# Expert rows added back as two fp32r parts behind the selections, and GpSimd's piece copy cut into four instructions of 512 columns

## The chip, the cores and the metric

The kernel runs on one core of a Trainium2 chip. The metric is the time of one launch in device microseconds: the median of three runs before is 1791.22 us (1789.27 to 1792.38). Lower is better.

## The reference

Two transformer blocks run one behind the other, all in float32, for one sequence of 256 tokens (16 meta tokens in front in the first block) of width 1024. The first block is a SwiGLU feed-forward, a mixer (stick-breaking attention and latent attention, each projected, gated and mixed by `w_out`) and a second SwiGLU. The second block is modulated by a condition vector and has a mixer (causal convolution and forgetting attention) and a mixture of 32 experts, four for each token. What matters here of the first mixer and of the experts:

```python
    g = jax.nn.sigmoid(gate_pre + b_gate)
    g_sb, g_mla = g[..., :D_MODEL], g[..., D_MODEL:]
    out = (g_sb * y_sb + g_mla * y_mla) @ w_out
    ...
    def expert_block(args):
        xi, e = args
        hc = xi @ w1[e] + b1[e]
        g, u = hc[:, :D_EXPERT], hc[:, D_EXPERT:]
        g = jnp.minimum(g, SWIGLU_LIMIT)
        u = jnp.clip(u, -SWIGLU_LIMIT, SWIGLU_LIMIT)
        hm = (u + 1.0) * (g * jax.nn.sigmoid(SWIGLU_ALPHA * g))
        return hm @ w2[e] + b2[e]
    ...
    y = jax.ops.segment_sum(yb.astype(jnp.float32) * gate_buf[:, None], tok_buf, num_segments=T)
```

After the experts comes the residual `x + g2 * y` and a last RMS norm with the gain `final_g`.

## The kernel before, in words

Each engine has its own program in one block, written out by hand, and they meet at semaphores. There is no scheduler: an engine does its instructions in the order of the text.

**Dense layers.** Activations lie with features on the 128 partitions and tokens in the columns. Weights come as a stream of pieces of 2048 columns (`PIECE`, 1 MB), into a ring of six slots on the SP queue. For precision a product is made as three fp32r products (lines 750 to 752): high and low parts of weights and inputs. ScalarE makes the high part of a piece (`split_piece`, L1537, into `w_hi`), VectorE the rest (`rest`, L2019, into `w_lo`; in the second mixer GpSimd, L1946). The table `BUF` says which of the buffers of `w_hi` and `w_lo` a piece takes. `split_piece` waits on `freed` for the last piece in the same buffer.

In the first mixer the attention ends with `MIX1_OUT`: eight pieces, four for the projections `o1` (two tiles of output columns a piece, 24 products a tile) and four for `w_out` (`w1`). VectorE's `gated` (L2324, L2325, L2327) multiplies the two projections of a tile by their gates and adds them, ScalarE copies the high part (`x_hi`, L1746), and VectorE makes the lower part (`x_lo`, L2071). ScalarE opens the gates by two sigmoids a tile (L1678, L1679). TensorE may begin tile m of `o1` when tile m - 2 is gated. `y_hi`, `y_lo`, `t_a` and `mtmp` lie in ring slots that double as the third weight buffer.

**Experts.** After routing, tokens are gathered in blocks of 64 slots. There is a block an expert, or more for one with more than 64 tokens. An expert's weights are 12 pieces, eight for `w_exp_in` and four for `w_exp_out`. SP loads them in pairs of 2 MB into four staging places (`stage_own`, `stage_conv`, `stage_gates`, `stage_norms`, L645), when GpSimd has emptied the place. GpSimd copies each piece into its slot of the ring of twelve (L1970), when it has landed and TensorE has freed the slot. The loops of TensorE (L1437), ScalarE (L1899) and VectorE (L2607) run over blocks.

A block on TensorE: bias (L1443), first layer for k = 0 to 3 (L1388), rows of the block before added back for half of the outputs (`back_to_tokens`, L1400), k = 4 to 7, the other half, the gather of the next block's tokens (L1366), transposes (L1457, L1378, L1464), and the second layer (L1477). Adding back is a product of the expert's output `ye` (64 slots on each half of the partitions) with the selection `ST` (slots by tokens, holding the gate's weight at the token of a slot), both fp32. ScalarE copies `ST` (L1910) and `ye` (L1912) out of PSUM. VectorE makes the selections `S` (L2572) and `SG` (L2614), one-hot rows for the bias (L2576), adds the sums to `acc` (`add_up`, L2583), and clips and multiplies the hidden layer. Behind the loop lie the last two adds, residual, squares, the norm's sum and root, and eight products by gain and root (L2642).

## Time and profile before

| | us |
|---|---|
| median of three runs | 1791.22 |
| profiled execution | 1787.52 |
| its span, first to last instruction | 1785.7 |
| PE busy | 1725.7 (97%) |
| DVE busy | 971.7 (54%) |
| POOL (GpSimd) busy | 840.2 (47%) |
| ACT busy | 528.4 (30%) |
| median from issue to landing of a staged pair | 15.4 |

PE is TensorE's matmuls, PEld its weight loads, SPq the transfers' queue. The span is time on the device between the first and the last instruction, and the profiled time has 1.8 us around it. A busy time sums the durations of an engine's instructions; for matmuls the ends are modelled, so they overlap. The HBM traffic is 560 MB, of which the experts' weights are 403 MB.

### The profile page before, as it was taken

How to read it: one execution, taken by the hardware profiler on the slowest of the kernel's cores; microseconds unless marked ns; L12 is line 12 of the kernel's file. 1: busy time of each engine (PE TensorE's matmuls, PEld its weight loads, DVE VectorE, ACT ScalarE, POOL GpSimd, SP SyncE). 2: the span in 40 equal slices, each digit the busy share in tenths (PEclk: the TensorE clock that was granted, in tenths of full speed). 3: DMA queues.
4: the chain of work that ended last, by engine and by line, in shares of the span. 5: the costliest groups of instructions: out<-in, count | busy, mean ns of one | idle time of the engine just before them, and what ended most of it. 6: DMA issues, size and time to landing. Idle time of an engine off the chain costs nothing.

```text
span 1785.7 us, 29478 instructions
## 1 busy us (share of the span) xinstructions
PE 1725.7 (97%) x10968; PEld 1097.3 (61%) x10969; DVE 971.7 (54%) x1438; ACT 528.4 (30%) x830; POOL 840.2 (47%) x492
## 2 busy tenths in 40 slices
PE   8999998998999999999999999999999999999997
PEld 8999996888899988898433333333333333333333
DVE  6777664576777666966654344334444435444334
ACT  6444444645644455573110110110101011010111
POOL 0000011000000038675677777777777768777773
PEclk9999999999999999999999999999999999999999
DMA  9767633225276625349799999999999999999994
GB/s 370 278 253 294 230 119 129 108 104 215 108 282 258 239 100 218 132 142 363 294 429 429 428 428 428 428 428 429 428 428 428 428 424 430 428 429 429 428 429 180
DMA packets 55262, 560.44 MB, mean 314 GB/s; under 512 B 6208, under 2 KB 7360, under 8 KB 14400
## 3 DMA queue, kind: packets, MB, share of 16 engines
q1 hardware_dynamic: 54912, 559.50, 77.1%
q8 instruction: 43, 0.70, 0.2%
q14 instruction: 19, 0.16, 0.0%
q10 hardware_dynamic: 288, 0.07, 0.0%
HBM read 558.50 MB, written 1.05 MB: 313 GB/s over the span
## 4 chain that ended last, share of the span: by engine, by line
PE 61%; DMA 22%; ACT 5%; DVE 5%; issue 4%; POOL 3%; POOLq 0%; SPq 0%; DVEq 0%; ACTq 0%
DMA stage_conv<-w_exp_in 14%; PE bank L1388 13%; PE bank L750 11%; PE bank L752 10%; PE bank L751 10%; DMA stage_conv<-w_exp_out 7%; PE bank L1477 6%; POOL ring L1970 3%; PE bank L1400 2%; PE bank L1366 2%; ACT w_hi L1537 1%; DVE bank L2000 1%; DMA ring<-stream 1%; PE bank L877 1%; PE bank L1378 1%
## 5 line engine op out<-in xcount | busy, mean ns | idle before, releaser
L1388 PE MATMUL bank<-ring,arena 128*64 128x512 f32 x2112 | 472.7, 596 | 11.5 <-POOL ring L1970 11.0
L750 PE MATMUL bank<-x_hi,w_hi 128*128 128x256 f32 (+1 forms) x1336 | 383.8, 287 | 18.5 <-DVE x_lo L2000 6.0
L752 PE MATMUL bank<-x_hi,w_lo 128*128 128x256 f32 (+1 forms) x1336 | 378.9, 284 | 0.0
L751 PE MATMUL bank<-x_lo,w_hi 128*128 128x256 f32 (+1 forms) x1336 | 378.5, 283 | 0.0
L1388 PEld LDWEIGHTS bank<-ring,arena 128*64 128x64 f32 x2112 | 143.4, 136 | 304.6 <-issue 243.0
L1946 POOL TENSOR_TENSOR w_lo<-ring,w_hi 128x512 fp32r<-128x512 f32 x104 | 135.1, 1334 | 386.4 <-ACT w_hi L1537 386.4
L750 PEld LDWEIGHTS bank<-x_hi,w_hi 128*128 128x128 f32 x1336 | 251.9, 189 | 26.6 <-issue 13.0
L752 PEld LDWEIGHTS bank<-x_hi,w_lo 128*128 128x128 f32 x1336 | 252.2, 189 | 0.0
L751 PEld LDWEIGHTS bank<-x_lo,w_hi 128*128 128x128 f32 x1336 | 251.4, 188 | 0.2
L1537 ACT ACTIVATE w_hi<-ring 128x2048 fp32r<-128x2048 f32 (+1 forms) x123 | 224.4, 1825 | 87.6 <-PE bank L750 83.1
L2019 DVE TENSOR_TENSOR w_lo<-ring,w_hi 128x2048 fp32r<-128x2048 f32 x91 | 208.1, 2286 | 75.1 <-ACT w_hi L1537 75.0
L1477 PE MATMUL bank<-ring,arena 128*64 128x512 f32 x1056 | 232.2, 592 | 0.0
L1970 POOL COPY ring<-stage_own 128x2048 f32<-128x2048 f32 x94 | 175.4, 1895 | 82.5 <-PE bank L1388 50.9
L1970 POOL COPY ring<-stage_conv 128x2048 f32<-128x2048 f32 x94 | 175.8, 1893 | 55.1 <-DMA stage_conv<-w_exp_in 23.2
L1970 POOL COPY ring<-stage_norms 128x2048 f32<-128x2048 f32 x92 | 171.9, 1893 | 62.1 <-DMA stage_norms<-w_exp_in 23.2
L1970 POOL COPY ring<-stage_gates 128x2048 f32<-128x2048 f32 x92 | 171.6, 1894 | 43.1 <-DMA stage_gates<-w_exp_in 21.6
L2576 DVE TENSOR_SCALAR onehot<-cst 96x64 bf16<-96x64 f32 x66 | 66.0, 1000 | 204.6 <-PE bank L1400 204.6
L1901 ACT ACTIVATE cst<-cst 128x512 f32<-128x512 f32 x33 | 20.8, 629 | 504.0 <-DVE cst L2004 504.0
L1477 PEld LDWEIGHTS bank<-ring,arena 128*64 128x64 f32 x1056 | 74.0, 137 | 136.1 <-issue 128.6
L2572 DVE TENSOR_SCALAR arena<-cst,small 128x64 f32 x66 | 68.2, 1076 | 139.1 <-issue 139.1
L1925 POOL TENSOR_TENSOR arena<-x_hi,x_lo 128x128 f32<-128x128 f32 x1 | 2.4, 2447 | 226.6 <-DVE x_lo L2000 226.6
L752 PE MATMUL bank<-hid_hi,w_lo 128*128 128x272 f32 (+1 forms) x352 | 100.0, 284 | 0.0
(384 smaller groups left out, 2225.8 us busy)
## 6 DMA issues: line engine op xcount, KB each, us to landing
ring<-stream SPq DMA_DIRECT2D x119, 1024.0 KB, 5.6
stage_own<-w_exp_in SPq DMA_DIRECT2D x31, 2048.0 KB, 15.4
stage_conv<-w_exp_in SPq DMA_DIRECT2D x31, 2048.0 KB, 15.4
stage_gates<-w_exp_in SPq DMA_DIRECT2D x31, 2048.0 KB, 15.4
stage_norms<-w_exp_in SPq DMA_DIRECT2D x31, 2048.0 KB, 15.4
stage_own<-w_exp_out SPq DMA_DIRECT2D x16, 2048.0 KB, 15.4
stage_conv<-w_exp_out SPq DMA_DIRECT2D x16, 2048.0 KB, 15.4
stage_gates<-w_exp_out SPq DMA_DIRECT2D x15, 2048.0 KB, 15.4
```

Of the source, the lines that this page charges most:

```text
L750: begin = mm(out_, wh, xh, start=start, stop=False)
L751: mm(out_, wh, xl, start=False, stop=False)
L752: return begin, mm(out_, wl, xh, start=False, stop=stop)
L1366: last = mm(to[pr, :], S[:, t, :], h2n[:, t, 512 * j:512 * j + 512], start=(t == 0), stop=(t == 1), tile_position=pos)
L1388: last = mm(bank[2 + gu][pr, :], xT[:, k % 4, k // 4, :], ring[:, k, c0:c0 + 512], start=False, stop=(k == KD - 1), tile_position=pos)
L1477: last = mm(bank[5][pr, :], hmT[:, k % 4, k // 4, :], ring[:, s, c0:c0 + 512], start=False, stop=(k == KD - 1), tile_position=pos)
L1537: last = A(w_hi[:, BUF[p], part * n:part * n + n], ring[:, p % RING, part * n:part * n + n], ACT.Copy)
L1946: nc.gpsimd.tensor_tensor(w_lo[:, BUF[p], c:c + REST_COLS], ring[:, p % RING, c:c + REST_COLS], w_hi[:, BUF[p], c:c + REST_COLS].bitcast(f32),
L1970: nc.gpsimd.tensor_copy(ring[:, j, :], stage[pair % PLACES][:, j % 2, :]).then_inc(in_place, 1)
L2019: tt(w_lo[:, BUF[p], :], ring[:, p % RING, :], w_hi[:, BUF[p], :].bitcast(f32), ALU.subtract)\
L2572: last = V.tensor_scalar(S[:, t, :], slots(b_), slot[:, t, bass.ds(e_, 1)], None, ALU.is_equal)
L2576: return V.tensor_scalar(to[0:3 * E, :], const("ones", 0, SLOT_TOK, 3 * E), cst[0:3 * E, bass.ds(e_ + CONST["eye3"][0], 1)], None, ALU.mult)
```

## The change

1. `BUF` for the first mixer's gates and outputs takes three buffers in turn. What lay in the third (`t_a`, `t_a_meta`, `mtmp`) and in the twelfth ring slot (`y_hi`, `y_lo`) now lies in `stage_own`.
2. ScalarE splits `MIX1_OUT[1]` ahead of the last `pair_evac`, and `MIX1_OUT[2]` behind three of the eight pairs of sigmoids. VectorE's `rest` of the following piece stands beside a gated tile, ahead of the lower parts. The first two tiles of `w1` are made together, k by k.
3. Adding rows back is two fp32r products: `ye_hi` and `ye_lo` against `ST`, which now holds ones. The gate's weight is taken up by `ye` as a factor a slot (`row_gate`, the row sum of the selection). VectorE makes `row_gate` and `ST` at the block's end, and `ye_lo` (`lower_rows`) behind the selections `S` and `SG`. TensorE waits for `m_yl` ahead of the add.
4. Behind the loop, `acc` takes up residual and gate first, the sums are added from PSUM, the gain is multiplied in ahead of the root, and two products of 1024 columns with the root follow.
5. GpSimd copies a piece in four instructions of 512 columns; the last one signals.

```diff
-for _p in MIX1_GATES:
-    BUF[_p] = (_p - MIX1_GATES[0] + 1) % 2
-BUF.update(zip(MIX1_OUT, (1, 0, 1, 0, 1, 0, 1, 2)))
+BUF.update(zip(MIX1_GATES, (1, 0, 1, 2, 0, 1, 2, 0)))
+BUF.update(zip(MIX1_OUT, (1, 2, 0, 1, 2, 0, 1, 2)))
...
@@ TensorE
-            for m in range(KD):
-                if m >= 2:
-                    pe.wait_ge(evac["w1"], m - 1)
-                tile(cur, bank[4 + m % 2][:, 0:SEQ], (lambda k: split_x(k, 0, SEQ)) if m else
-                     lambda k: split_x_first("w1", k, 0, SEQ), KD, proj)
+            two_tiles(cur, [bank[4 + i][:, 0:SEQ] for i in range(2)], "w1", w_lower, ORDER[cur.b // BLK] + 1)
+            for m in range(2, KD):
+                pe.wait_ge(evac["w1"], m - 1)
+                tile(cur, bank[4 + m % 2][:, 0:SEQ], lambda k: split_x(k, 0, SEQ), KD, proj)
...
                     for j, _, pr in halves:
-                        mt = 2 * r + mp
-                        last = mm(bank[banks[j]][:, mp * 256:mp * 256 + 256], ye[pr, mt * P:mt * P + P],
-                                  ST[pr, :, :].rearrange("p a b -> p (a b)"),
-                                  start=True, stop=True, tile_position=(64 * j, 0))
+                        to = bank[banks[j]][:, mp * 256:mp * 256 + 256]
+                        mm(to, ye_hi[pr, mt * P:mt * P + P], ST[pr, :], start=True, stop=False,
+                           tile_position=(64 * j, 0))
+                    for j, _, pr in halves:
+                        to = bank[banks[j]][:, mp * 256:mp * 256 + 256]
+                        last = mm(to, ye_lo[pr, mt * P:mt * P + P], ST[pr, :], start=False, stop=True,
+                                  tile_position=(64 * j, 0))
...
-                pe.wait_ge(m_ys, g + 1)
+                pe.wait_ge(m_yl, g + 1)
...
@@ ScalarE
+            split_piece(MIX1_OUT[1])
+            use(ACT.Sigmoid)
             pair_evac(3, yy_hi, soft["mla"]["pv"], soft["mla"]["y"])
-            split_piece(MIX1_OUT[1])
-            open_gates("gates", graw)
+            open_gates("gates", graw, range(0, 3))
+            split_piece(MIX1_OUT[2])
+            open_gates("gates", graw, range(3, KD))
             for m in range(KD):
                 if m % 2 == 0 and m:
-                    split_piece(MIX1_OUT[m // 2 + 1])
+                    split_piece(MIX1_OUT[m // 2 + 2])
...
-                act.wait_ge(m_xt, g + 2)
-                act.wait_ge(m_comb, g * 2 + 2)
-                A(ST[:, :, :].rearrange("p a b -> p (a b)"), bank[0][:, 0:256], ACT.Copy).then_inc(m_sts, 1)
+                act.wait_ge(m_sts, g + 2)
                 act.wait_ge(m_y, g + 1)
-                A(ye, bank[5][:, :], ACT.Copy).then_inc(m_ys, 1)
+                A(ye_hi[:, :], bank[5][:, :], ACT.Copy, scale=row_gate).then_inc(m_ys, 1)
...
@@ GpSimd
-                    nc.gpsimd.tensor_copy(ring[:, j, :], stage[pair % PLACES][:, j % 2, :]).then_inc(in_place, 1)
+                    for c in range(0, PIECE, MOVE_COLS):
+                        last = nc.gpsimd.tensor_copy(ring[:, j, c:c + MOVE_COLS],
+                                                     stage[pair % PLACES][:, j % 2, c:c + MOVE_COLS])
+                    last.then_inc(in_place, 1)
...
@@ VectorE
                     if m:
                         then(m - 1)
+                    beside(m)
                 then(KD - 1)
...
+            def lower_rows(g):
+
+                dve.wait_ge(m_ys, g + 1)
+                stt(ye_lo[:, :], bank[5][:, :], row_gate, ye_hi[:, :].bitcast(f32), ALU.mult, ALU.subtract)\
+                    .then_inc(m_yl, 1)
...
+                lower_rows(g)
                 dve.wait_ge(m_comb, g * 2 + 1)
...
+                V.reduce_sum(row_gate, bank[0][:, 0:256], AX.X)
+                ts(ST[:, :], bank[0][:, 0:256], 0.0, None, ALU.is_gt).then_inc(m_sts, 1)
+            dve.wait_ge(m_acc, n_blocks * 2 + 1)
+            for m in range(KD):
+                mark(stt(acc[:, m, :], acc[:, m, :], mod[:, 40 + m:41 + m], real(res[:, m, :]), ALU.mult, ALU.add))
+            lower_rows(n_blocks)
...
+            for half in range(2):
+                four = slice(half * KD // 2, (half + 1) * KD // 2)
+                tt(fin[:, four, :], acc[:, four, :], rstd[:, 0:SEQ].unsqueeze(1).to_broadcast([P, KD // 2, SEQ]),
+                   ALU.mult).then_inc(fin_ready, KD // 2)
```

The order on ScalarE at the start of the output projections, before:

```order
L1707 ACTIVATE y_mla_hi<-bank 128x256
L1537 ACTIVATE w_hi<-ring 128x2048
L1512 ACT_TABLE_LOAD
L1678 ACTIVATE arena<-arena,col 128x256
L1679 ACTIVATE arena<-arena,col 128x256
...
L1746 ACTIVATE x_hi<-arena 128x256 x2
L1537 ACTIVATE w_hi<-ring 128x2048
```

And of the change (lines from here on are ten higher on this engine: L1547 is the split, L1688 and L1689 the sigmoids):

```order
L1547 ACTIVATE w_hi<-ring 128x2048
L1522 ACT_TABLE_LOAD
L1717 ACTIVATE y_mla_hi<-bank 128x256
L1688 ACTIVATE arena<-arena,col 128x256
L1689 ACTIVATE arena<-arena,col 128x256
...
L1547 ACTIVATE w_hi<-ring 128x2048
L1688 ACTIVATE arena<-arena,col 128x256
L1689 ACTIVATE arena<-arena,col 128x256
...
L1759 ACTIVATE x_hi<-arena 128x256 x2
L1547 ACTIVATE w_hi<-ring 128x2048
```

The first split went ahead of the last y, the second from behind sixteen sigmoids and two x_hi to behind six sigmoids.

VectorE at the same place, before:

```order
L2019 TENSOR_TENSOR w_lo<-ring,w_hi 128x2048
L2324 TENSOR_TENSOR ring<-bank,arena 128x256
L2325 TENSOR_TENSOR ring<-bank,arena 128x256
L2327 TENSOR_TENSOR arena<-ring 128x256
...
L2071 TENSOR_TENSOR x_lo<-arena,x_hi 128x256
L2019 TENSOR_TENSOR w_lo<-ring,w_hi 128x2048
L2324 TENSOR_TENSOR ring<-bank,arena 128x256
```

And of the change:

```order
L2031 TENSOR_TENSOR w_lo<-ring,w_hi 128x2048
L2336 TENSOR_TENSOR stage_own<-bank,arena 128x256
L2337 TENSOR_TENSOR stage_own<-bank,arena 128x256
L2339 TENSOR_TENSOR arena<-stage_own 128x256
L2031 TENSOR_TENSOR w_lo<-ring,w_hi 128x2048
...
L2083 TENSOR_TENSOR x_lo<-arena,x_hi 128x256
L2336 TENSOR_TENSOR stage_own<-bank,arena 128x256
```

The rest (L2019, now L2031) of the piece for columns 4 and 5 moved from behind the second gated tile and the first x_lo to directly behind the first gated tile.

VectorE in the loop over expert blocks, of the change: the selections, the lower rows, the one-hot row, the add to `acc`, and at the block's end the row sum and `ST`:

```order
L2583 TENSOR_SCALAR arena<-cst,small 128x64
L2633 ISA x2
L2633 TENSOR_SCALAR arena<-cst,small 128x64 x2
...
L2012 SCALAR_TENSOR_TENSOR ye_lo<-bank,small,ye_hi 128x512
L2635 ISA
L2587 ISA
L2587 TENSOR_SCALAR onehot_77<-cst 96x64
L2594 TENSOR_TENSOR arena<-arena,bank 128x512 x2
...
L2650 COPY arena<-bank 128x512
L2651 TENSOR_REDUCE small<-bank 128x1
L2016 TENSOR_SCALAR ST<-bank 128x256
```

Before, the three rows L2012, L2651 and L2016 were not there, and ScalarE copied `ST`.

## Rows read from the trace of the kernel before

**Rows 1.** The page: GB/s in the 40 slices; the expert matmuls of the first layer.
```profile
GB/s 370 278 253 294 230 119 129 108 104 215 108 282 258 239 100 218 132 142 363 294 429 429 428 428 428 428 428 429 428 428 428 428 424 430 428 429 429 428 429 180
L1388 PE MATMUL bank<-ring,arena 128*64 128x512 f32 x2112 | 472.7, 596 | 11.5 <-POOL ring L1970 11.0
```

**Rows 2.** Windows: length, busy us (records) of each engine, clock, DMA share, GB/s.
```profile
500.00:600.00 100.00, 100.00 (x848) 100.00 (x847) 70.80 (x89) 45.63 (x53) 0.00 (x0) 1.00 0.73 267
852.00:855.00 3.00, 2.49 (x32) 2.34 (x32) 1.89 (x9) 1.11 (x2) 0.00 (x0) 1.00 0.05 22
1600.00:1700.00 100.00, 99.66 (x502) 36.11 (x500) 38.50 (x57) 8.96 (x16) 76.00 (x41) 1.00 1.01 428
```

**Rows 3.** GpSimd's timeline, expert stage: start, us, what.
```profile
1656.41 3.73 POOL L1970 COPY ring<-stage_own 128x2048 f32<-128x2048 f32 x2 [1.16 <-PE bank L1477]
1661.30 3.73 POOL L1970 COPY ring<-stage_conv 128x2048 f32<-128x2048 f32 x2 [1.16 <-DMA stage_conv<-w_exp_in]
```

**Rows 4.** The chain that ended last: start, us, what.
```profile
1471.30 6.87 PE bank L1388 x32
1478.17 1.06 PE bank L1400 x8
...
1498.40 6.86 PE bank L1388 x31
...
1762.07 6.90 PE bank L1477 x32
```

**Rows 5.** Timeline of the end, GpSimd, ScalarE and VectorE.
```profile
1759.18 3.73 POOL L1970 COPY ring<-stage_conv 128x2048 f32<-128x2048 f32 x2 [1.14 <-DMA stage_conv<-w_exp_out]
...
1768.99 0.60 ACT L1912 ACTIVATE arena<-bank 128x512 f32<-128x512 f32 x1 [6.75 <-PE bank L1477]
...
1775.11 1.67 DVE L2000 SCALAR_TENSOR_TENSOR arena<-arena,small,res 128x256 f32<-128x256 f32 x4
...
1779.09 3.26 DVE L2000 SCALAR_TENSOR_TENSOR arena<-arena,col,rstd 128x256 f32<-128x256 f32 x8 [2.30 <-ACT rstd L1527]
```

**Rows 6.** Timeline of the first mixer's output projections.
```profile
404.12 0.49 ACT L1679 ACTIVATE arena<-arena,col 128x256 f32<-128x256 f32 x1
404.52 0.71 ACT L1746 ACTIVATE x_hi<-arena 128x256 fp32r<-128x256 f32 x2
405.13 1.90 ACT L1537 ACTIVATE w_hi<-ring 128x2048 fp32r<-128x2048 f32 x1
...
407.06 2.29 DVE L2019 TENSOR_TENSOR w_lo<-ring,w_hi 128x2048 fp32r<-128x2048 f32 x1 [1.68 <-ACT w_hi L1537]
...
410.54 0.39 PE L750 MATMUL bank<-y_sb_hi,w_hi 128*128 128x256 f32 x1 [4.27 <-DVE arena L2327]
...
431.13 0.36 PE L750 MATMUL bank<-x_hi,w_hi 128*128 128x256 f32 x1 [0.30 <-DVE w_lo L2019]
```

**Rows 7.** Groups by form, GpSimd: count, busy us, mean ns, idle before.
```profile
L1970 POOL COPY ring<-stage_conv 128x2048 f32<-128x2048 f32 x94 | 175.8, 1893 | 55.1 <-DMA stage_conv<-w_exp_in 23.2 <-DMA stage_conv<-w_exp_out 12.7 <-PE bank L1388 9.8
L1946 POOL TENSOR_TENSOR w_lo<-ring,w_hi 128x512 fp32r<-128x512 f32 x104 | 135.1, 1334 | 386.4 <-ACT w_hi L1537 386.4
L1933 POOL COPY arena<-arena 64x64 f32<-64x64 f32 x1 | 0.2, 235 | 0.1
```

**Rows 8.** Timeline of the first expert block, TensorE, VectorE and the transfers' queue.
```profile
862.91 0.33 SPq L645 DMA_DIRECT2D stage_own<-w_exp_out  x1
...
863.21 0.73 PEld L1400 LDWEIGHTS bank<-arena 64*128 64x128 f32 x8 [0.81 <-issue]
863.52 1.40 DVE L2572 TENSOR_SCALAR arena<-cst,small 128x64 f32 x2 [4.70 <-issue]
...
864.84 2.62 DVE L2614 TENSOR_SCALAR arena<-cst,small 128x64 f32 x4
...
871.28 0.36 SPq L645 DMA_DIRECT2D stage_gates<-w_exp_in  x1
...
879.30 0.34 SPq L645 DMA_DIRECT2D stage_norms<-w_exp_in  x1
```

More of the change, by code:

```diff
@@ L224, in build @@
         slot_bytes = PIECE * 4
-        stage = [at_place("stage_own", [P, 2, PIECE])[0],
+        stage_own, own_at = at_place("stage_own", [P, 2, PIECE])
+        own = stage_own[:, :, :].rearrange("p a b -> p (a b)")
+        stage = [stage_own,
                  at_place("stage_conv", [P, 2, PIECE], over=arena_at)[0],
@@ L290, in build @@
         gate = sm_area.take(2, E)
+        row_gate = sm_area.take(1)
         slot = sm_area.take(2, E)
@@ L574, in build @@
         m_y = sem("m_y")
-        m_ys = sem("m_ys")
+        m_ys = sem("m_y_high")
+        m_yl = sem("m_y_lower")
         m_comb = sem("m_comb")
@@ L1481, in _ @@
                 last.then_inc(m_y, 1)
-            pe.wait_ge(m_ys, n_blocks + 1)
+            pe.wait_ge(m_yl, n_blocks + 1)
             pe.wait_ge(m_sts, n_blocks + 1)
@@ L2314, in _, with gated @@
             rest(MIX1_OUT[1])
-            def gated(n, gr, tmp, to, then=lambda m: None):
+            def gated(n, gr, tmp, to, then, beside=lambda m: None):
                 for m in range(KD):
```

83 lines of the change are left out of this document (42 added, 41 removed).

## The prediction

> **What bounds the kernel now.** I read the page first [rows 1]: from the 21st of 40 slices on its line of GB/s stands flat at 424 to 430. So there are two regimes: up to about 852 us the dense layers, bound by TensorE, and then the 32 experts. In the windows [rows 2] the dense feed-forward issues 848 matmuls in 100 us, 0.118 us apart and at full clock, the DMA engines rest between 852 and 855 us (share 0.05, all places full), and in the expert stage they are busy throughout (share 1.01 from 1600 to 1700 us), where VectorE works 38.5 of 100 us; TensorE's 99.66 there say little, since the ends of matmuls are modelled. The GpSimd timeline [rows 3] then gives the beat of the expert stage: two pieces (one pair, 2 MB) are copied every 4.89 us, 3.73 us of it busy and 1.16 us idle until the next pair lands. Twelve pieces make an expert, so an expert takes 29.4 us, set by the transfers. TensorE alone needs 27.1 us for a block (1471.30 to 1498.40 in the chain, [rows 4]). It falls a block behind at the one expert that has two blocks (33 blocks in all: the 2112 records of L1388 in rows 1 are 64 a block) and makes up 2.3 us a block from there. At the end it still lags: the last pair's copy starts at 1759.18 and ends at 1762.91 [rows 5], while the last layer's matmuls, begun at 1762.07, run until 1768.97 [rows 4]. Behind the last piece only a quarter of that layer has to follow, 1.72 us, so the lag is 1768.97 - (1762.91 + 1.72) = 4.3 us. From 1768.97 to the end of the span, 16.7 us are a tail in which nothing else runs.
>
> **The change, part by part.**
>
> **1. First mixer, output projections.** Before [rows 6], ScalarE runs all sixteen sigmoids, then x_hi at 404.52, and only then splits the piece for columns 4 and 5 (405.13, 1.90 us); VectorE stands behind that split (rest at 407.06, 2.29 us), its third gated tile comes behind that, and TensorE, which needs it, starts column 4 at 410.54 after 4.27 us idle. Further on it starts the third w1 tile at 431.13. Now the order is another, and w_hi/w_lo have three buffers instead of two in turn, so a split waits for no reader. I played the queues forward with durations of rows 6 (ACT split 1.90, sigmoids 0.40 apart, DVE rest 2.29, and, of three operations of 256 columns, a gated tile 1.3 with its waits) and 24 x 0.118 = 2.84 us of TensorE a tile. The split for columns 2 and 3 moves ahead of the last y evacuation; three sigmoid pairs end at 397.3, the split for columns 4 and 5 at 399.2, its rest at 401.5, the third gated tile at 405.3, before TensorE ends column 3 (405.8). Then 0.6 us of waiting at column 5 remains and 0.1 at column 7; o1 ends at 418.0. The first two w1 tiles now go together, k by k, so they start while x_split 6 and 7 (421.4, 422.2) are still to come, and end at 423.7; the third waits for ScalarE's evacuation (0.7 us) and starts at 424.4. That is **6.7 us** earlier than 431.13. Bounds: 4.3 (the one stall only) and 8. What TensorE does up to the next norm is unchanged, and a shift here moves everything behind it.
>
> **2. Rows added back, in the loop.** Eight records of 256-column fp32 took 1.06 us on the chain [rows 4], twice a block. Eight fp32r matmuls of 256 columns, in pairs on the two halves of the rows, would be 4 x 0.107 = 0.43 us if paired as before; unpaired 8 x 0.118 = 0.94. I take 0.6: a block falls from 27.1 to about 26.2 us. This buys nothing where transfers set the beat; it only has to remove the 4.3 us of lag, and twelve blocks behind the double one are enough for it with 0.4 us each. VectorE gains the row sum, the selection and the lower half (256, 256 and 512 columns; some 1.4 us a block, estimated from the 2.29 for 2048 in rows 6), ScalarE loses a copy; VectorE is idle for more than half of the stage [rows 2], so these hide. If that cover went, the next tokens' selection would be late next, and behind it TensorE's gather.
>
> **3. GpSimd's four copies.** One piece of 2048 columns took 1.893 us and the smallest warm copy (64 columns, 64 partitions) 0.235 [rows 7]: 0.836 ns a column and 0.18 us fixed. So 512 columns should last 0.61 us, 0.56 apart, because like instructions overlap by 0.05 us here (two large copies take 3.73, not 3.79, [rows 3]). A pair then costs 8 x 0.56 = **4.5 us against the beat of 4.89**. Lower bound 3.73 (overheads hidden), upper bound 8 x 1.33 = 10.7 from the two-input subtraction of 512 columns; I go by the copies, being the same operation. By the Trainium skill, GPSIMD Engine Reference, "Instruction dispatch", every instruction is broadcast and dispatched in software by each of the eight cores, which speaks against cutting one into four. With the fixed part paid in full and no overlap the pair would cost 4.9, just at the beat (by that rule). In the sum, the last pair comes into place 0.75 us later (4.5 for 3.73), and all others are hidden by the 0.4 us of slack.
>
> VectorE's small selections are why the copies are cut: its 64-column operations last 0.24 us alone, but 1.40 us for two and 2.62 for four while copies run [rows 8]. It mostly ends in time, so a shorter wait alone is worth nothing.
>
> **4. The first block, a new wait.** TensorE's row add now waits for the lower rows (m_yl), which VectorE makes behind its selections. In block 0 VectorE only reaches these at 863.52 and 864.84 [rows 8], after its registers are loaded, and TensorE starts the row add at 863.21. With the shorter copies the six selections end at 866.5 (six waits of at most 0.56), the subtraction at 867.2: a stall of 3.9 us, 3.5 net of the faster add. Queued behind it are the expert matmuls of k = 4 to 7, which free the slots GpSimd fills, and on the SP queue the transfers that wait for those copies, just when the DMA engines restart from idle. The issues at 862.91, 871.28 and 879.30 become about 863.7, 875.9 and 882.7. From the last on the stream is unbroken, so it ends 882.7 - 879.3 = **3.4 us** later. That is a real loss, as the stream has no slack anywhere behind.
>
> **5. End of the loop.** Last pair at 1759.18 + 3.4 = 1762.6, in place at 1767.1, last matmul at 1768.9; by the other path, from piece 7 through add, gather and the 6.9 us layer, 1769.1. Against 1768.97: **0.1 us later**, the lag of 4.3 being what pays for parts 3 and 4.
>
> **6. Tail.** From the last matmul: ScalarE's high half 0.63, VectorE's lower half 0.74, row add 0.75, eight 256-column operations 3.3 (the 3.26 of rows 5), squares, sum and root behind them 2.3 (1776.78 to 1779.09), then two products of 1024 columns at 1.14 (half of 2.29 in rows 6) and 3.3 for the last store (from 1782.35). Sum 13.3 against 16.7: **3.4 us saved**. The eight multiplications by the gain fit beside squares, sums and root (2 us against 2.3).
>
> **Sum**: -6.7 + 0.1 - 3.4 = **-10.0 us**. The profiled execution took 1787.52 us (span 1785.7 and 1.8 around), so 1777.5 for a like one; the median of the runs shown is 1791.22, 3.7 above it. I forecast the median: 1791.2 - 10.0 = **1781.2**.
>
> **The rivals.**
> - *The first block costs nothing.* The lower rows come in time, or the stream restarts as before. For it: the DMA engines have just drained, and part of the first issues is bound by the copies anyway. Against it: 863.21 is before 863.52. Then 3.5 more: 1777.7.
> - *The mixer gives only its large stall*, ScalarE's queue being late elsewhere. Some 5 us less: 1786.
> - *The stream cannot close up.* With 0.4 us slack a pair, any copy held up by VectorE opens a further gap in the restart; 6 to 7 us lost: 1788, about the same as before.
> - *GpSimd becomes the bound (the slower side).* Point of decision: 4.894 / 8 = 0.612 us from copy to copy. With a gap of 0.04 behind each in place of an overlap it is 0.65, a pair 5.2, and 186 pairs x 0.31 = 57 us less the 10 gained: 1838. For it: the margin is 8%, and VectorE's eight small operations an expert (0.24 each) may now hold up copies. By the Trainium skill, SBUF — State Buffer, "Who interferes with whom", the port pair of the two engines is locked for a whole instruction, whichever comes first; the 1.40 and 2.62 us agree on VectorE's side. Against it: pairs of copies take 3.73 whatever VectorE does, and even 8 x 0.24 = 1.9 us on top of 26.9 an expert stays under 29.4.
> - *The change does nothing on the path*: excluded only in the expert stage, whose beat I expect untouched.
>
> **How the numbers follow.** Forecast 0.50 (own range 1777 to 1785), no cost of the first block 0.15, smaller mixer gain 0.12, stream not closed 0.10, GpSimd the bound 0.13. A measurement of this kernel can tell about 0.2%, 3.6 us. The first three are faster, the fourth is split, the fifth slower: faster 0.78, same 0.08, slower 0.14. The range 1774 to 1789 takes in the first four with the bounds of part 1 (4.3 to 8) and leaves out GpSimd's case.
>
> **What would show it.** In the changed profile: no wait of some 4 us in o1 and the third w1 tile near 424; a TensorE wait of 3 to 4 us for ye_lo in the first block, and a second full stop of the DMA engines there; copies of 0.61 us, pairs of 4.5 every 4.89; row adds of some 0.6 us; a last layer that waits for GpSimd; 13 us from the last expert matmul to the end. Pairs that follow each other more than 4.9 us apart with GpSimd never idle would prove me wrong, as would a first block without that wait.

## The result and the profile after

The changed kernel takes 2017.9 us (median of 4 runs) beside 1790.2 us of the kernel before on the same chip: ratio 1.127, 95% interval 1.126 to 1.129. It is **227.7 us slower**; the forecast was 10 us faster, with a range up to 1789.

The page of the profiled execution (span 2016.6 us; GB/s in 40 slices of 50.4 us; first costliest group of section 5: line, engine, operation, shapes, count, busy us, mean ns, idle before):

```profile
PE 1764.1 (87%) x10968; PEld 1121.8 (56%) x10969; DVE 1284.1 (64%) x1545; ACT 518.2 (26%) x797; POOL 976.5 (48%) x1608
GB/s 370 266 252 287 172 104 126 105 199 171 290 240 147 188 126 147 334 336 325 368 345 347 373 322 371 334 355 378 321 368 331 220 371 374 324 367 336 354 353 21
L2587 DVE TENSOR_SCALAR onehot<-cst 96x64 bf16<-96x64 f32 x66 | 383.6, 5812 | 211.3 <-PE bank L1411 211.3
```

The flat 428 GB/s of [rows 1] have become 220 to 378, so the transfers no longer set the beat. TensorE has lost its load too: 85.4 of 100 us from 1600 to 1700 where it had 99.7 [rows 2]. What stands at the top is an operation that the prediction never priced by itself: VectorE's one-hot, 64 columns, now 5.8 us on average. The page of the kernel before has it at 1.0 us:

```profile
L2576 DVE TENSOR_SCALAR onehot<-cst 96x64 bf16<-96x64 f32 x66 | 66.0, 1000 | 204.6 <-PE bank L1400 204.6
```

GpSimd's groups by form, which the forecast did price:

```profile
L1980 POOL COPY ring<-stage_conv 128x512 f32<-128x512 f32 x376 | 212.6, 613 | 145.2 <-PE bank L1487 140.6 <-PE bank L1394 4.6
```

A copy lasts 0.613 us, as forecast (0.61), and eight of them 4.50 us, as forecast. GpSimd is not the bound: it stands idle for 8.8 or 9.4 us at a time in 29 blocks. What TensorE waits for (us in total, times, longest):

```profile
PE bank L1407 <- DVE arena L2594: 209.0, 29, 7.2
PE bank L1407 <- DVE ye_lo L2012: 5.6, 2, 3.9
```

One block in the changed kernel, VectorE first, then GpSimd, then TensorE (start us, us, what, idle before and its releaser):

```profile
1625.52 12.82 DVE L2587 TENSOR_SCALAR onehot<-cst 96x64 bf16<-96x64 f32 x1 [6.55 <-PE bank L1411]
1638.25 1.27 DVE L2594 TENSOR_TENSOR arena<-arena,bank 128x512 f32<-128x512 f32 x2
...
1613.76 4.50 POOL L1980 COPY ring<-stage_own 128x512 f32<-128x512 f32 x8
1618.21 4.51 POOL L1980 COPY ring<-stage_conv 128x512 f32<-128x512 f32 x8
1622.65 4.51 POOL L1980 COPY ring<-stage_gates 128x512 f32<-128x512 f32 x8
1627.11 4.50 POOL L1980 COPY ring<-stage_norms 128x512 f32<-128x512 f32 x8
1631.56 4.51 POOL L1980 COPY ring<-stage_own 128x512 f32<-128x512 f32 x8
1636.01 2.28 POOL L1980 COPY ring<-stage_conv 128x512 f32<-128x512 f32 x4
1647.67 0.61 POOL L1980 COPY ring<-stage_conv 128x512 f32<-128x512 f32 x1 [9.38 <-PE bank L1487]
...
1639.58 0.58 PE L1407 MATMUL bank<-ST,ye_hi 64*128 64x256 f32 x2 [7.22 <-DVE arena L2594]
```

This is the main part of the loss in one picture, a circle of three engines. The one-hot is issued at 1625.52, while GpSimd copies without a break, and ends at 1638.33, 0.05 us after the last copy (1636.01 + 2.28). It has stood across 22 boundaries between two copies, where [rows 8] had let every operation in at the first. Behind it on VectorE waits the sum (L2594), and for that TensorE's second row add, 7.2 us. TensorE frees no slots meanwhile, so GpSimd fills the ring and stops; only that lets VectorE in. While TensorE catches up, the staging places fill as well. So GpSimd finds four pairs ready when it resumes and again copies without a break, into the next one-hot: the state keeps itself going. 29 blocks have a one-hot of 12.8 us. From one expert to the next GpSimd now needs 35.5 and 36.1 us in turn where it needed 29.4, and from its first pair to its last 1122.3 us (854.28 to 1976.60) where it needed 900.0 (859.16 to 1759.18, the latter in [rows 5]): **+222.3 us, nearly all of the loss**. Once the circle broke: at the expert with two blocks GpSimd waited 24 us for a slot, and the next four one-hots took 0.25, 0.24, 0.70 and 2.48 us. Then came the one at 1625.52.

The wait of 7.2 us is not all that a block loses. Within each of these stops TensorE's granted clock falls to half (0.50, the level of 1.2 GHz) and stays there for a while behind it, for example from 1635.6 to 1645.6 and from 1673.1 to 1679.8 us, of which TensorE works for 6.0 and 4.1 us; between the two it is 1.00. By an estimate from these rows this costs 3.0 and 2.0 us a block. An undisturbed block of 26.3 us, the wait of 7.2 and these 2.5 on average make 36.0, beside the 35.5 and 36.1 measured. So more than a third of the 6.4 us by which a block exceeds the beat comes with the slow stretch. No run here takes the clock's part away by itself.

### The profile page after: what moved, and what is told of

It is laid out like the page before. It is cut to its first block, busy times and chain, and to the rows that moved or that the text cites. A ratio compares the mean times of both kernels' runs of the same rounds, so it can differ in the third digit from the quotient of the medians.

```text
span 2016.6 us, 30667 instructions
## 1 busy us (share of the span) xinstructions
PE 1764.1 (87%) x10968; PEld 1121.8 (56%) x10969; DVE 1284.1 (64%) x1545; ACT 518.2 (26%) x797; POOL 976.5 (48%) x1608
## 4 chain that ended last, share of the span: by engine, by line
PE 69%; DVE 14%; issue 11%; ACT 4%; DMA 1%; POOL 1%; DVEq 0%; SPq 0%; ACTq 0%
PE bank L1394 12%; PE bank L1487 11%; PE bank L757 10%; PE bank L759 10%; PE bank L758 10%; DVE onehot L2587 9%; PE bank L1372 5%; PE bank L1407 2%; DVE arena L2594 2%; PE bank L1411 1%; PE bank L1384 1%; DVE bank L2012 1%; DMA ring<-stream 1%; PE bank L1467 1%; ACT w_hi L1547 1%
## 5 line engine op out<-in xcount | busy, mean ns | idle before, releaser
L2587 DVE TENSOR_SCALAR onehot<-cst 96x64 bf16<-96x64 f32 x66 | 383.6, 5812 | 211.3 <-PE bank L1411 211.3
L1980 POOL COPY ring<-stage_conv 128x512 f32<-128x512 f32 x376 | 212.6, 613 | 145.2 <-PE bank L1487 140.6
L1980 POOL COPY ring<-stage_norms 128x512 f32<-128x512 f32 x368 | 208.1, 613 | 127.5 <-PE bank L1487 127.5
L757 PEld LDWEIGHTS bank<-x_hi,w_hi 128*128 128x128 f32 x1336 | 252.7, 189 | 24.4 <-issue 12.5
L2031 DVE TENSOR_TENSOR w_lo<-ring,w_hi 128x2048 fp32r<-128x2048 f32 x91 | 208.0, 2286 | 64.2 <-ACT w_hi L1547 63.9
L1547 ACT ACTIVATE w_hi<-ring 128x2048 fp32r<-128x2048 f32 (+1 forms) x123 | 224.4, 1825 | 83.1 <-PE bank L757 78.6
L1407 PE MATMUL bank<-ST,ye_hi 64*128 64x256 f32 x272 | 53.5, 402 | 214.6 <-DVE arena L2594 209.0
L1980 POOL COPY ring<-stage_own 128x512 f32<-128x512 f32 x376 | 211.8, 613 | 56.3 <-PE bank L1394 56.3
L1980 POOL COPY ring<-stage_gates 128x512 f32<-128x512 f32 x368 | 207.3, 613 | 0.5 <-PE bank L1394 0.5
L1407 PEld LDWEIGHTS bank<-ST,ye_hi 64*128 64x128 f32 x272 | 32.9, 238 | 271.1 <-DVE arena L2594 234.5
L1372 PE MATMUL bank<-arena 128*64 128x512 f32 x272 | 112.7, 977 | 0.0
## 6 DMA issues: line engine op xcount, KB each, us to landing
stage_own<-w_exp_out SPq DMA_DIRECT2D x16, 2048.0 KB, 10.2
```

The source lines that it names most:

```text
L757: begin = mm(out_, wh, xh, start=start, stop=False)
L1372: last = mm(to[pr, :], S[:, t, :], h2n[:, t, 512 * j:512 * j + 512], start=(t == 0), stop=(t == 1), tile_position=pos)
L1407: mm(to, ye_hi[pr, mt * P:mt * P + P], ST[pr, :], start=True, stop=False, tile_position=(64 * j, 0))
L1547: last = A(w_hi[:, BUF[p], part * n:part * n + n], ring[:, p % RING, part * n:part * n + n], ACT.Copy)
L1980: last = nc.gpsimd.tensor_copy(ring[:, j, c:c + MOVE_COLS], stage[pair % PLACES][:, j % 2, c:c + MOVE_COLS])
L2031: tt(w_lo[:, BUF[p], :], ring[:, p % RING, :], w_hi[:, BUF[p], :].bitcast(f32), ALU.subtract)\
```

## Experiments

All times are medians beside the kernel before on the same chip (1789.5 to 1790.4 us). Three questions: which part of the change costs, what shuts VectorE out, and how little removes it.

**1. whole_pieces: the change without the cut.**

```diff
-MOVE_COLS = 512
+MOVE_COLS = 2048
```

> The change with GpSimd's copies left whole (2048 columns), everything else of it kept. Theory L (lock-out): the loss comes from the cut alone. Copies of 512 columns follow each other so closely that VectorE's one-hot operation (96 x 64, to bf16) stands 12.8 us in 28 of 33 blocks, until the ring is full and GpSimd stops; TensorE waits 7.2 us for it (209 us in all). Whole copies let it in after 1.9 us at most, so the time is 1790.2 - 4.9 (dense layers, as measured) - 2.2 (tail, 14.5 for 16.7 us) + 0 to 3, so 1782 to 1786, and no wait of TensorE for the sum of VectorE's L2594 over 1 us. Theory R (row add): the new place of the lower rows moves the one-hot into a phase of the copies in which it loses; then whole copies also leave long one-hots (several times 1.9 us) and the time stays over 1820.

Measured: 1783.6 us, ratio 0.9966 (0.9952 to 0.9979). The one-hot in its profile:

```profile
L2587 DVE TENSOR_SCALAR onehot<-cst 96x64 bf16<-96x64 f32 x65 | 53.9, 829 | 171.2 <-PE bank L1411 171.2
```

Theory L holds. Everything else of the change together gains 6 us; the cut costs some 234.

**2. split_alone: the kernel before with only the copy cut into four.** The loop over four copies of 512 columns in place of the single copy, nothing else.

> The kernel before with nothing but the copy of a piece cut into four of 512 columns. Theory L: the one-hot operation stands until the ring is full here too, over 10 us in most blocks, and the time is 1950 to 2060. Theory R: without the new row add the one-hot waits for one copy of 0.61 us at most, the pairs take 4.5 us against a beat of 4.89, and the time is 1788 to 1793.

Measured: 2039.2 us, ratio 1.139 (1.137 to 1.141); 29 one-hots of 12.5 us, and TensorE waits 199.8 us for the sum. The new row add is not needed for the loss. Theory R is out.

**3. add_first: the addition ahead of the one-hot.**

```diff
                 dve.wait_ge(m_comb, g * 2 + 1)
-                one_hot(onehot2, e).then_inc(m_SG, 1)
                 dve.wait_ge(m_acc, g * 2 + 1)
                 add_up(0)
+                one_hot(onehot2, e).then_inc(m_SG, 1)
```

> The change with two steps of VectorE exchanged: the addition of the rows (from PSUM, two of 512 columns) goes ahead of the one-hot for the output bias. This moves the one-hot by about 1.2 us, so to another phase of the copies (0.556 us apart). Theory K (kind): an operation of this kind never gets in between two short copies, in whatever phase. Then it still stands for over 10 us in most blocks, TensorE now waits for hm instead of the sum, and the time stays at 1950 to 2060. Theory P (phase): the one-hot was locked out because it always came 0.08 us behind the start of a copy; in four blocks it came at 0.51 or 0.52 us and got in after 0.70. Then the long ones vanish in a part of the blocks or in all, and the time falls below 1900.

Measured: 1966.8 us. The one-hot still stood for 11.2 to 11.7 us in 29 blocks, and this at many phases of the copies (from 0.04 over 0.21 and 0.41 to 0.55 us behind a start). Phase does not decide. The stall fell less heavily because TensorE could go on to its second row add first: it now waits 148.5 us in all, ahead of the transposes, where it had waited 209.0 for the sum.

**4. onehot_float: the one-hot in fp32, turned to bf16 by ScalarE.** VectorE writes 96 x 64 fp32 into dead columns (the router's logits and mask), ScalarE copies them to `onehot1` and `onehot2`.

> The change with both one-hots written by VectorE as fp32 (as its selections are, which get in at every boundary of two short copies) and turned to bf16 by ScalarE. Theory K (the form of the operation, bf16 out, decides): no one-hot over 0.7 us, no wait of TensorE for the sum, time 1782 to 1788. Theory P (phase or place): VectorE's fp32 one-hot stands as long as the bf16 one did (12.8 us), time about 2018.

Measured: 2018.2 us, the same as the change to 0.3 us.

```profile
L2592 DVE TENSOR_SCALAR arena<-cst 96x64 f32<-96x64 f32 x65 | 385.9, 5936 | 209.1 <-PE bank L1412 209.1
```

So the type written does not decide either, and both theories I had set up were wrong or unhelpful: neither form nor phase. What was left to compare was how long GpSimd had been copying. In all profiles so far, an operation of VectorE's issued after up to 14 copies in a row had got in at the next boundary, and one issued after 23 or more never. The selections always fell in the first group and the one-hot in the second.

**5. onehot_early: the one-hot moved ahead, directly behind the lower rows.**

```diff
                 lower_rows(g)
-                dve.wait_ge(m_comb, g * 2 + 1)
                 one_hot(onehot2, e).then_inc(m_SG, 1)
+                dve.wait_ge(m_comb, g * 2 + 1)
```

> The change (copies of 512 columns kept) with the one-hot for the output bias moved up by some 7 us, directly behind the lower rows. In the steady state it then comes some 12 copies after GpSimd last stood still, where the selections come and get in, and not 25. Theory A (age of the run of copies decides: up to 14 copies in a row VectorE got in at the next boundary, from 23 on never): the one-hot lasts at most 0.7 us, TensorE waits for nothing of VectorE's, the time is 1782 to 1788. Theory K (the selections get in because of their own form, 128 partitions and a comparison, and the one-hot does not): it stands from the earlier place until the ring is full, and the time is over 1950.

Measured: 1855.7 us, between the two expectations. VectorE's timeline of one block, with the first and the second one-hot:

```profile
944.61 0.54 DVE L2587 TENSOR_SCALAR onehot<-cst 96x64 bf16<-96x64 f32 x1
...
959.45 13.59 DVE L2587 TENSOR_SCALAR onehot<-cst 96x64 bf16<-96x64 f32 x1
```

The moved one-hot, issued behind 13 copies, gets in at once: the same operation, so theory K is out. But the block's other one-hot, which had met an idle GpSimd before, now comes after 39 copies in a row and is shut out for 13.6 us in 15 blocks (and for 2.1 to 2.6 us, until GpSimd stops, in 14 more). The stall had moved on, a thing I should have looked for: TensorE waits 55.8 us for it.

**6. half_pieces: copies of 1024 columns.** `MOVE_COLS = 1024`.

> The change with copies of 1024 columns, two a piece. By the lengths of 512 (0.61) and 2048 columns (1.89) one should last 1.04 us, a pair 3.9 to 4.0. Theory A (number of copies in a row): after the same 14 us only 14 of them have run, so the one-hot gets in at the next boundary, 1.1 us at most, and the time is 1782 to 1787. Theory T (time without a stop decides, some 8 to 12 us): it stands until GpSimd stops in many blocks, and the time is over 1900.

Measured: 1784.1 us, ratio 0.9963 (0.9949 to 0.9977), copies of 1.043 us, pairs of 4.00 us, no one-hot over 1.14 us. Theory T is out as it stood. One detail spoke against theory A as well: two one-hots came after 22 copies without a stop, and got in (0.53 and 0.62 us).

**7. wait_piece: GpSimd waits for its own last copy behind every piece.**

```diff
                     last.then_inc(in_place, 1)
+                    pool.wait_ge(in_place, SLOTS + j + 1 if it is None
+                                 else it * (2 * SLOTS) + (n + 1) * SLOTS + j + 1)
```

> The change with copies of 512 columns and one wait more: behind every piece (four copies) GpSimd waits until the last of them is complete, so that it never has more than four copies in a row. Theory A: every one-hot gets in at the end of a piece at the latest, 2.3 us at most, and mostly after 0.7; TensorE's waits for the sum vanish. The waits cost GpSimd 0.05 to 0.25 us a piece, a pair takes 4.6 to 5.0 us against the beat of 4.89: the time is 1782 to 1805. Theory D (GpSimd is dispatched too slowly anyway, whatever VectorE does): pairs over 5.5 us, over 1880.

Measured: 1857.2 us, ratio 1.038; no operation of the one-hot's kind over 0.72 us.

```profile
1602.58 2.31 POOL L1980 COPY ring<-stage_conv 128x512 f32<-128x512 f32 x4 [0.24 <-POOL ring L1980]
1605.13 2.29 POOL L1980 COPY ring<-stage_conv 128x512 f32<-128x512 f32 x4 [0.24 <-POOL ring L1980]
...
1618.60 2.29 POOL L1980 COPY ring<-stage_own 128x512 f32<-128x512 f32 x4 [1.06 <-issue]
```

A stop of 0.24 us is enough to let VectorE in. But a piece now takes 2.53 us and a pair 5.06, over the beat of 4.89, and at each expert the stop in which GpSimd loads a register with the number of blocks is 0.8 us longer than the others (1.06 for 0.24): 31.4 us an expert. This is the rival that I had called "GpSimd becomes the bound", made on purpose, and dearer than the 1805 I expected at most.

**8. one_try: the two engines alone.** One kernel with 34 runs of copies:

```python
# GpSimd, in each run
last = nc.gpsimd.tensor_copy(ring[:, j, c:c + cols], stage[:, j % 2, c:c + cols])
if i == at - 1:
    last.then_inc(reached, 1)
# VectorE
dve.wait_ge(reached, n + 1)
last = V.tensor_scalar(onehot[0:96, :], cst[0:96, 0:64], cst[0:96, 128:129], None, ALU.mult)
```

> A kernel of its own that computes nothing of the model and stores zeros: GpSimd copies in runs (48 copies of 512 columns, 34 of 1024, 17 of 2048, 64 of 256) out of SBUF into SBUF, and in each run VectorE tries one small operation once, when copy number N of the run is complete (the form of the one-hot, 96 x 64 to bf16, or of the selection, 128 x 64). No transfers and no matmuls run beside it. Theory A: with 512 columns the operation lasts at most 0.7 us up to N = 15 and until the end of the run (over 5 us) from N = 23 on, for both forms alike. Theory K: only the one-hot is ever shut out. Theory X (it needs more than the two engines, such as the transfers): none lasts longer than one copy. For 1024 and 2048 columns theory A expects no long one up to N = 14; for 256 columns the long ones begin at the same N of 15 to 23.

Its timeline of VectorE, for copies of 512 columns behind 11, 13, 15 and 17 copies, then the selection behind 11 and 15, then 1024 columns behind 11 and 15:

```profile
70.75 0.57 DVE L67 TENSOR_SCALAR onehot<-cst 96x64 bf16<-96x64 f32 x1 [28.62 <-POOL ring L53]
98.82 0.57 DVE L67 TENSOR_SCALAR onehot<-cst 96x64 bf16<-96x64 f32 x1 [27.50 <-POOL ring L53]
126.90 18.42 DVE L67 TENSOR_SCALAR onehot<-cst 96x64 bf16<-96x64 f32 x1 [27.50 <-POOL ring L53]
154.97 17.30 DVE L67 TENSOR_SCALAR onehot<-cst 96x64 bf16<-96x64 f32 x1 [9.66 <-POOL ring L53]
...
367.31 0.57 DVE L69 TENSOR_SCALAR S<-cst 128x64 f32<-128x64 f32 x1 [28.62 <-POOL ring L53]
396.50 18.42 DVE L69 TENSOR_SCALAR S<-cst 128x64 f32<-128x64 f32 x1 [28.62 <-POOL ring L53]
...
574.11 1.00 DVE L67 TENSOR_SCALAR onehot<-cst 96x64 bf16<-96x64 f32 x1 [36.60 <-POOL ring L53]
611.71 18.72 DVE L67 TENSOR_SCALAR onehot<-cst 96x64 bf16<-96x64 f32 x1 [36.60 <-POOL ring L53]
```

Behind up to 13 copies a try gets in at the next boundary; behind 15 or more it stands until the run of 48 ends, each two copies later shortening it by just 1.12 us. Both forms behave alike, and no transfer or matmul is needed: theories K and X are out. The size hardly matters: with 2048 columns a try behind 11 (after 20 us) gets in and one behind 14 does not; with 256 columns one behind 7 does and behind 15 (5 us) does not. It is a number of copies, not a time. (Only with 256 columns were those shut out let in before the run's end, all at the 38th copy; why is open.)

**9. many_tries: several tries in a run.** The same kernel, with a list of copies that VectorE tries behind, and other kinds of operation and of stops in some runs.

> Again a kernel of its own that stores zeros; runs of 48 copies of 512 columns, and now with more than one try in a run. In one_try a single try got in behind copy 13 and was shut out to the run's end behind copy 15, for all sizes and both forms. Theory A1 (the count runs from GpSimd's last stop): tries behind copies 7, 15, 23, 31, 39 are shut out from the second on; 11 and 23: the second is shut out. Theory A2 (the count runs anew when VectorE has got in): the tries every 8 and every 10 copies all get in (0.6 to 0.7 us), 11 and 23 too, and 7 and 27 does not. A single try behind 12 gets in, behind 14 one or the other. Tries that read PSUM are never shut out and, by A2, do not start the count anew if they do not need the port. A semaphore wait and increment every four copies (as the expert loop has) change the count little. With a real stop (a wait for its own copy) every 12 or every 8 copies, tries behind 15, 23 and 31 all get in.

| tries behind copies | what it lasted (us) |
|---|---|
| 12; 14 | 0.57; 18.9 (to the end) |
| 7, 15, 23, 31, 39 | 0.50, then 0.57 each |
| every 4 from 7 to 43 | 0.50, then 0.57 each |
| 11, 21 (and 31, 41, reached while the second stood) | 0.50, 15.1 (to the end) |
| 11, 23; 7, 27 | the second to the end |
| 13, 24 | 19.5 (to the end) |
| 11 reading PSUM, 15 from SBUF | 0.22, 18.4 (to the end) |
| 15, two inputs from SBUF | 18.4 (to the end) |
| 15 and 23, a memset | 0.11 |
| 11; 15; 23 with a semaphore every 4 copies | 0.50; 18.4; 13.9 |
| 15 or 23, with a real stop every 12 or 8 copies | 0.25 to 0.50 |

Theory A2 holds and A1 is out: the count starts anew when VectorE has got in, but from there it is shorter. Every 8 copies it gets in; 10 copies behind the last it no longer does (11, 21), which I had not expected. After a stop of GpSimd 12 are let pass, 14 are not, and 13 went both ways (let in when issued 0.03 us behind the end of the 13th, shut out when issued 0.11 us behind it). A very short stop is enough: without one, each copy starts 0.06 us before the end of the last by the trace, and with the wait for the own last copy 0.06 us behind it. An operation that reads PSUM and writes SBUF is never shut out and does not start the count anew. A memset is not shut out either. Semaphore steps between copies change nothing.

**10. wait_pair: the stop behind every pair only.** As wait_piece, but `if j % 2:`.

> The change with copies of 512 columns and a wait of GpSimd for its own last copy behind every pair only (eight copies; wait_piece had one behind every four, 0.24 us each, and pairs of 5.06 us). Both theories of the count (it starts anew when GpSimd stops, or also when VectorE has got in) expect no operation of VectorE's over 0.75 us, since eight in a row are below every count that shut it out (11 and more). A pair takes 4.50 + 0.28 = 4.78 us, below the beat of 4.89, and with 0.8 us for GpSimd's register at each expert 29.5 against 29.37 us: 1784 to 1792, against 1857 of wait_piece. If the extra wait itself costs more than its 0.24 us (theory W, what it takes GpSimd to fill up again), pairs pass 4.89 and the time is over 1800.

Measured: 1802.5 us, ratio 1.0075 (1.006 to 1.009), a miss of 10 us. Every operation got in (0.72 us at most), so the mechanism is right and the price was not. The experts take 29.4 and 29.8 us in turn, on average 0.2 over the beat, some 6 us in all. The larger part is what the slack had been there for: before, the experts behind the start and behind the one with two blocks take 27.1 to 28.2 us and win back what was lost; here none is below 29.4.

**11. half_lower_first: copies of 1024 columns, the lower rows first.**

```diff
                 e, b = where(g)
+                lower_rows(g)
                 e_next, b_next = where(g + 1)
...
-                lower_rows(g)
                 dve.wait_ge(m_comb, g * 2 + 1)
```

> The change with copies of 1024 columns, and VectorE makes the lower rows between the registers of this block and those of the next, ahead of the selections. Theory F: this takes away TensorE's wait of 3.6 us for ye_lo in the first block, the transfers' issues at 866.3, 871.6 and 879.2 us come 3 us earlier, and the stream and the time end as much earlier: 1780 to 1781.5 where half_pieces had 1784.1. In the other blocks the selections then end some 6 us later (about 9 us behind the start of the block), still ahead of the gather that reads them. Rival G: selections, one-hot and sum are late there, TensorE waits a little in every block, and the time is 1784 or more. Rival H: the restart of the stream is bound by the copies, so the wait goes and the time stays at 1783 to 1785.

Measured: **1779.3 us, ratio 0.9945 (0.9931 to 0.9959)**, faster than both kernels. Theory F holds by the trace: from the first expert matmul to the last it takes 911.2 us where half_pieces took 918.4. The medians alone would not settle it, since the intervals of the two ratios overlap (0.9931 to 0.9959 and 0.9949 to 0.9977), and not all of the difference is the first block's: the dense layers ended 1.8 us earlier here, and the tail took 1.4 us more, as its 16 matmuls for the norm took 5.2 us in place of 3.7. TensorE's first block in half_pieces, then in this kernel:

```profile
860.99 0.58 PE L1407 MATMUL bank<-ST,ye_hi 64*128 64x256 f32 x2 [3.56 <-DVE ye_lo L2012]
...
862.15 9.37 PE L1394 MATMUL bank<-ring,arena 128*64 128x512 f32 x32
```

```profile
855.59 0.39 PE L1407 MATMUL bank<-ST,ye_hi 64*128 64x256 f32 x2
...
856.25 7.09 PE L1394 MATMUL bank<-ring,arena 128*64 128x512 f32 x32
```

The wait of 3.56 us is gone, and so are 2.3 us behind it: the 32 matmuls take 7.09 us again, not 9.37. In the window from 852 to 870 us the granted clock is 0.81 in half_pieces and 1.00 here. More closely, it is 0.50 in half_pieces from 860.0 to 866.7 us (the level of 1.2 GHz, a pair of matmuls every 0.85 us in place of 0.43) and 1.00 behind that. So the clock fell within the stop of TensorE (858.6 to 862.2 us) and was low for 4.6 us behind it, and without the stop it did not fall.

**12. keep_trying and keep_closer: VectorE given more to do.** The change as it is, GpSimd's code untouched, and four useless small operations a block, 128 x 32 from SBUF to SBUF. The second kernel has two of them one slot earlier (in the cut below, the lines with a minus are the first kernel's):

```diff
+            def small_try(g, n, freed_slots=None):
+                if freed_slots is not None:
+                    dve.wait_ge(freed, g * SLOTS + (DENSE + RING + freed_slots))
+                dve.wait_ge(masked, g * 4 + n + 1)
+                V.tensor_scalar(lgt[:, 0, :], const("ones", 0, E), const("one"), None, ALU.mult).then_inc(masked, 1)
...
                 lower_rows(g)
-                small_try(g, 0, 3)
+                small_try(g, 0, 2)
...
                 add_up(0)
-                small_try(g, 1, 7)
+                small_try(g, 1, 6)
```

> The change exactly as it is (copies of 512 columns, GpSimd untouched), and four small operations of VectorE's more in every block, whose results nobody reads (128 x 32 from SBUF to SBUF), placed so that VectorE never leaves the port alone for more than 8 copies (4.5 us): when the third and the seventh slot are freed, behind gl, and behind the block's last operation. Theory A2 (VectorE is shut out when neither a stop of GpSimd nor an operation of its own came within the last 8 to 13 copies): all of them get in, no one-hot lasts over 0.75 us, TensorE waits for no sum, and the time falls from 2018 to 1782 to 1787, although VectorE has more to do. If only GpSimd's stops counted (A1), or if it were VectorE's load that costs, the one-hot or one of the new operations stands until the ring is full, and the time stays over 1950.

Measured: 2025.3 us, no gain. The first of the new operations was itself shut out:

```profile
890.53 14.39 DVE L2631 TENSOR_SCALAR arena<-cst 128x32 f32<-128x32 f32 x1 [4.96 <-PE bank L1394]
```

It came 10 copies behind the last selection, where I had meant 8 at most; a slot's release is counted one step late. By many_tries 10 is too far, so this told nothing against A2, but nothing for it.

> keep_trying with two of its four small operations one slot earlier. There the first of them came 10 copies after VectorE's last selection had got in (6 us, not the 4.5 meant, since a slot's release is counted one step late) and stood for 14.4 us; many_tries had shut out a try 10 copies after the last and let in tries 8 copies apart. Now it comes 7 copies after, and every other gap is 4 to 7 copies. Theory A2: all get in, no operation of VectorE's between SBUF and SBUF over 0.75 us, TensorE waits for no sum, 1782 to 1790. Theory A1 (only GpSimd's stops count): an operation from the age of 15 copies on stands until the ring is full, and the time stays over 1950.

Measured: **1786.4 us, ratio 0.9979 (0.9969 to 0.9988)**: 231.5 us less than the change, by four more operations a block on the engine that was late.

```profile
887.79 0.54 DVE L2631 TENSOR_SCALAR arena<-cst 128x32 f32<-128x32 f32 x1 [3.24 <-PE bank L1394]
888.24 4.50 POOL L1980 COPY ring<-stage_gates 128x512 f32<-128x512 f32 x8
891.07 0.61 DVE L2587 TENSOR_SCALAR onehot<-cst 96x64 bf16<-96x64 f32 x1 [2.74 <-PE bank L1411]
```

No operation from SBUF lasts over 0.75 us, although GpSimd twice makes 100 copies in a row. That settles it inside the real kernel: copies of 512 columns are fast enough, and what counts is how many of them pass between two that VectorE gets in.

## Why the prediction was wrong, point by point

- **Bounds of the kernel before** (the transfers' beat of 4.89 us, TensorE 2.3 us faster a block): right. half_pieces and whole_pieces keep the 29.4 us an expert.
- **Part 1, mixer**: direction right, size 4.9 us for 6.7. The stall of 4.27 us is gone, but the third w1 tile starts at 426.2, not 424.4. I moved TensorE at full clock throughout. Now its granted clock is 0.66 in the window from 395 to 400 us, where column 0 starts (matmuls 0.21 us apart, not 0.12); in the kernel before, a dip of the same size (0.66) stood at 410 to 415, behind the stall, and so looked like a part of it.
- **Part 2, row add**: right. It takes 0.67 us (1572.00 to 1572.68), and an undisturbed block 26.3 us.
- **Part 3, the four copies: the step that failed.** Length, spacing and pair (0.613, 0.556, 4.50 us) came out as forecast. The sentence beside them did not: that VectorE "mostly ends in time, so a shorter wait alone is worth nothing", which put the wait for the one-hot at nothing. I took for granted that more boundaries mean more chances to get in, and took from [rows 8] that an operation waits for one copy. Those rows held copies of 1.84 us of which at most 8 followed each other before GpSimd stopped; the rule "one boundary, then in" ends behind some 13, and cutting each by four gave runs of 48. I also named a rival in which VectorE holds up GpSimd, and none in which GpSimd holds up VectorE, although the row with 1.40 and 2.62 us showed just this direction. Its 13% on "GpSimd the bound" were not that case either: GpSimd stood idle for some 9 us in 29 blocks. The runs showed in place of the step: the one-hot stands 12.8 us in 29 blocks, TensorE waits 209.0 us for the sum behind it, and without the cut (whole_pieces) both are gone.
- The rule cited there (the Trainium skill, "SBUF — State Buffer", "Who interferes with whom": the port pair is locked for a whole instruction by whoever comes first) agrees with every wait of one copy, as with the 0.57 us behind 13 copies in one_try. One try that stands across 32 boundaries of later copies (18.4 us) goes beyond it: who had waited longest did not get in. The measurement decides. The forecast's other citation of the Trainium skill ("GPSIMD Engine Reference", "Instruction dispatch") names a cost of dispatch for every instruction; the runs show 0.13 us fixed for each copy, and that was in the sum.
- **Part 4, first block**: the wait came (3.9 us, forecast 3.9) and the stream was late by it, but by 5.7 us in place of 3.4. Measured from the first expert matmul, the fourth transfer is issued 23.1 us later before and 28.8 in half_pieces and whole_pieces. The difference is the clock behind the stop (9.4 and 9.6 us for 32 matmuls, not 7.1), which I had left out; half_lower_first gives both back (22.9).
- **Part 5, end of the loop**: forecast 0.1 us longer than before from the first expert matmul to the last. whole_pieces is 3.7 us longer and half_pieces 5.7. The 2.3 us just named are a part, and another is that the last layer ends 7.3 and 7.5 us behind the start of the last pair, not 6.5; some 2 us of half_pieces stay unexplained.
- **Part 6, tail**: 14.5 us, forecast 13.3, before 16.7: the order was right, and of the 1.2 us some small waits between the steps were missing, and the last store took 3.8 us, not 3.3.
- **Sum**: without the cut the forecast's -10.0 would have been -5.9 (medians of whole_pieces and the kernel before). The profiled executions show -3.2 up to the first expert matmul (853.0 for 856.2), +3.7 in the loop and -2.2 in the tail, -1.7 in all; the dense part varies, its end lies between 848.6 and 853.0 us in six profiles with the same instructions there. The range, 1774 to 1789, would have held that, not the likeliest value.

## What to carry to other kernels

When a long instruction on one engine is cut so that another engine gets in oftener, ask not only how long one piece is but how many follow each other without a stop, and look at the engine that waits to get in, not only at the one that copies. A wait seen in a trace holds only for the run lengths of that trace. And where three engines wait for each other in a circle (copies need slots, slots need matmuls, matmuls need the small operation that the copies shut out), a loss of a few us in one block refills the queue and so reproduces itself in the next, and here each stop of TensorE had a stretch at half clock on top; test a cure for where the stall moves.

## What the runs showed of the hardware

- VectorE's small operations from SBUF to SBUF (both forms of one input, and one of two) get in at the next boundary only while few copies of GpSimd have followed each other: 12 behind a stop in, 13 both ways, 14 and more out; behind an operation of VectorE's own that got in, 8 in, 10 out. It is a count, not a time: with 256, 1024 and 2048 columns (0.34 to 1.84 us a copy) the tries behind 7 or 11 copies got in and those behind 14 or 15 did not. Shut out, an operation stands until GpSimd stops (with 256 columns only until the 38th copy of the run).
- A gap of 0.06 us between two copies (a wait for the own last copy) starts the count anew, and a semaphore wait that is already met does not. Reading PSUM, or a memset, is free of it (0.22 and 0.11 us).
- What mechanism keeps this count was not found. That the traces show GpSimd's copies overlapping by 0.06 us may belong to it; that is only argued.
- A copy costs GpSimd 0.345, 0.558, 0.985 and 1.838 us from start to start for 256, 512, 1024 and 2048 columns: 0.13 us fixed and 0.83 ns a column.
- With the stop of TensorE of 3.6 us in the first block of half_pieces the granted clock fell to 0.50 for 6.8 us, so that the fourth transfer came 5.7 us later than before. With the stops of 7.2 us in the changed kernel it was 0.50 for 6.8 or 10.2 us, mostly in turn.
